# Long convolutions: taps of two channel tiles in turn, pair sums in column tiles, and two of the eight z units in the loop

## The chip, the cores and the metric

One core of one Trainium2 chip runs the kernel. The metric is the device time of one launch in microseconds (us); the median over the runs of the kernel before is given below. The engines are TensorE (PE in the rows), VectorE (DVE), ScalarE (ACT), GpSimd (POOL) and SyncE (SP), which issues the weight loads.

## The reference

The whole program is a chain of four mixers over x of 256 positions by 1024 channels, then a block of three attentions and a feed-forward part, all in float32. The change touches only the mixer of layers 0 and 3, the conformer convolution (E = 2048 inner channels, 31 taps):

```python
def conformer_conv_mixer(h, w_in, conv_w, conv_b, ln_g, ln_b, w_out):
    proj = h @ w_in
    val, glu_gate, z = jnp.split(proj, 3, axis=-1)
    u = val * jax.nn.sigmoid(glu_gate)
    u = causal_depthwise_conv(u, conv_w) + conv_b
    u = jax.nn.silu(layer_norm(u, ln_g, ln_b))
    return (u * jax.nn.silu(z)) @ w_out
```

The layer norm runs over the 2048 channels of a position, so its mean and variance are known only once all channels have been convolved.

## The kernel before

Channels lie on the 128 partitions and the 256 positions along the free axis, so the 2048 channels are 16 tiles (c = 0 to 15). Every engine has its own program and they meet by semaphores. The order of work is written out by hand in `conf_act`, `conf_pool`, `conf_dve` and `conf_pe`, once for each of the two convolutions (`j` = 0 and 1, called convolution 0 and 1 below).

**The loop.** For tile c PE computes the unit `vg[c]`: value and gate, 2 x 8 float32 matmuls of 256 columns (line 782; each is two passes, so two records in the trace). ACT takes the sigmoid of the gate (line 997) and DVE multiplies both into the padded buffer `up` (`gated`, line 1113). That multiply also frees the PSUM bank: `vg[c]` lies in bank 0 or 1, and the unit two places on takes the bank only then. The 31 taps are then split: DVE adds up 20 of them in two partial sums in a PSUM bank (lines 1141, 1139, 1144), ACT multiplies the other 11 (line 1026), through a ring of four buffers, and POOL adds these (line 1081), into `accp`, of which there are two. `join` adds the parts with two dependent additions (lines 1120 and 1121). From tile 3 on a `shift`, the mean of tile 0, goes into the partial sums to keep the variance accurate; tiles 0 to 2 get it afterwards (lines 1154, 1157).

**The sums.** For the layer norm PE multiplies a 128x128 block of ones by each convolved tile (line 1194, `sum_of`) and by its square from ACT (line 1200, `squares_of`): 32 float32 matmuls of 256 columns for a convolution, whose result stands in all 128 rows. DVE then works out mean and 1/std as 128x256 tiles (lines 1161 to 1172).

**z.** Eight units of z (2 x 8 matmuls each, line 782) are spread: one behind each of tiles 3, 7, 11 and 15, one among the last sums, and three (5, 6, 7) behind the last sum. ACT evicts them with silu (`conf_z`, line 976).

**The tail.** Tile by tile: DVE centres and scales (lines 1167, 1182), ACT takes silu (line 1052), POOL multiplies by silu(z) (line 1092), ACT writes the high part of y (line 955), DVE the low part (line 959). Behind z 7 PE starts the output product `out_pe` (lines 862 to 864, three one-pass matmuls for each k). Its first half-unit takes y tile by tile. An output unit is two half-units of 24 matmuls; for each, ACT must have copied the weights to `whi` (line 370) and DVE or POOL, by turns, must have written the rest to `wlo` (line 379). Four half-units fit into `whi`/`wlo`. In the tail ACT, POOL and DVE do these splits of the first units at fixed tiles: `AHEAD_BESIDE` and `OUT_BESIDE` put those of output unit 0 at tile 8, those of unit 1 and half of unit 2 at tile 13, and two more halves at tile 15. Units are loaded in the order of PE's use into a ring of three; a slot is loaded again once PE is through with it.

## Time and profile before

| | |
|---|---|
| median of 3 runs | 1503.85 us (1503.31 to 1507.31) |
| time of the profiled execution | 1504.31 us |
| its span, first to last instruction | 1502.5 us |
| mean granted TensorE clock | 0.998 |
| PE busy | 1476.4 us |
| DVE busy | 1074.9 us |
| ACT busy | 852.7 us |
| POOL busy | 499.7 us |

Busy time counts overlapping records once. Matmuls are pipelined, so the pace of a run of matmuls is read from the starts of two groups, not from the duration of one. In the timeline a row is a run of like instructions: start, time to the end of the last, engine, line, operation, tiles, count, and in brackets the idle time before it with the instruction that ended it.

### The profile page before, as it was taken

What the parts mean: (1) busy time and instruction counts of PE and PEld (TensorE: products, weight loads), DVE (VectorE), ACT (ScalarE), POOL (GpSimd) and SP (SyncE); (2) the same over time, 40 slices, a digit from 0 to 9 for tenths busy, and PEclk for the clock granted to TensorE, in tenths of its full rate; (3) what the DMA queues carried; (4) which work ended last, traced back from release to release, by engine and by line L of the source; (5) the groups of instructions that cost most, each with busy time, mean ns of one, the idle gap of its engine ahead of it and who ended that gap; (6) DMA issues with size and microseconds to landing.
All of it is one profiled execution on the core that took longest, in us unless ns stands there. A gap on an engine that the chain in (4) does not pass through costs nothing.

```text
span 1502.5 us, 25334 instructions
## 1 busy us (share of the span) xinstructions
PE 1476.4 (98%) x9411; PEld 1329.7 (88%) x9411; DVE 1074.9 (72%) x2235; ACT 852.7 (57%) x1604; POOL 499.7 (33%) x459
## 2 busy tenths in 40 slices
PE   8999999999999999999999999999999999999999
PEld 6888899998889988889988888989888878988887
DVE  5899966546787698887599997656247667786632
ACT  4676666545565555555456676545336655555542
POOL 2777642433333200000057785154421112000033
PEclk9999999999999999999999999999999999999999
DMA  7554454666644568866444444654753223576653
GB/s 206 149 148 139 139 197 157 223 173 150 138 144 142 157 187 210 218 196 196 144 136 141 141 141 162 189 141 134 214 153 93 78 85 113 168 197 190 177 191 116
DMA packets 308109, 239.40 MB, mean 159 GB/s; under 512 B 18017, under 2 KB 286707, under 8 KB 307988
## 3 DMA queue, kind: packets, MB, share of 16 engines
q1 hardware_dynamic: 295816, 228.70, 52.3%
q10 hardware_dynamic: 12172, 9.10, 2.6%
q8 instruction: 75, 1.23, 0.4%
q14 instruction: 46, 0.38, 0.1%
HBM read 236.02 MB, written 1.75 MB: 158 GB/s over the span
## 4 chain that ended last, share of the span: by engine, by line
PE 79%; DVE 14%; ACT 3%; SPq 1%; DMA 1%; issue 1%; POOL 1%; DVEq 0%; ACTq 0%; POOLq 0%
PE bank L782 15%; PE bank L802 12%; PE bank L804 6%; PE bank L862 3%; DVE bank L1144 3%; PE bank L864 3%; PE bank L863 3%; PE bank L1660 3%; PE bank L1662 3%; PE bank L1661 3%; PE bank L1287 2%; DVE wlo L379 2%; PE bank L825 2%; PE bank L761 1%; PE bank L763 1%; PE bank L762 1%
## 5 line engine op out<-in xcount | busy, mean ns | idle before, releaser
L379 POOL TENSOR_TENSOR wlo<-ring,whi 128x1024 fp32r<-128x1024 f32 x101 | 252.3, 2504 | 843.6 <-ACT whi L370 843.6
L370 ACT CAST whi<-ring 128x1024 fp32r<-128x1024 f32 x330 | 338.3, 1046 | 188.6 <-PE bank L1662 49.5
L379 DVE TENSOR_TENSOR wlo<-ring,whi 128x1024 fp32r<-128x1024 f32 (+1 forms) x229 | 291.6, 1293 | 150.8 <-ACT whi L370 150.1
L782 PE MATMUL bank<-sqb,ring 128*128 128x256 f32 x1504 | 330.3, 379 | 1.0 <-DMA ring<-in_a_w_in_dram 1.0
L782 PEld LDWEIGHTS bank<-sqb,ring 128*128 128x128 f32 x1504 | 285.7, 190 | 40.9 <-DMA ring<-in_a_w_in_dram 1.1
L802 PE MATMUL bank<-xhl,whi 128*128 128x512 f32 x768 | 269.1, 395 | 1.3 <-DVE xhl L707 1.3
L1081 POOL TENSOR_TENSOR scratch<-scratch 128x256 f32<-128x256 f32 x288 | 200.2, 732 | 107.3 <-ACT scratch L1026 96.6
L1144 DVE SCALAR_TENSOR_TENSOR bank<-scratch,convw,bank 128x256 f32<-128x256 f32 x576 | 231.1, 482 | 0.0
L804 PE MATMUL bank<-xhl,wlo 128*128 128x256 f32 x768 | 215.3, 280 | 0.0
L802 PEld LDWEIGHTS bank<-xhl,whi 128*128 128x128 f32 x768 | 144.0, 188 | 34.8 <-issue 2.1
L1026 ACT ACTIVATE scratch<-scratch,convw 128x256 f32<-128x256 f32 x320 | 144.2, 498 | 22.4 <-POOL scratch L1081 21.8
L862 PE MATMUL bank<-y_hi,whi 128*128 128x256 f32 x512 | 146.2, 286 | 2.4 <-POOL wlo L379 2.4
L804 PEld LDWEIGHTS bank<-xhl,wlo 128*128 128x128 f32 x768 | 145.3, 189 | 0.0
L863 PE MATMUL bank<-y_lo,whi 128*128 128x256 f32 x512 | 145.0, 283 | 0.0
L864 PE MATMUL bank<-y_hi,wlo 128*128 128x256 f32 x512 | 145.0, 283 | 0.0
L1660 PE MATMUL bank<-xhl,whi 128*128 128x256 f32 x384 | 110.3, 287 | 0.8 <-DVE qk L1620 0.8
L1661 PE MATMUL bank<-xhl,whi 128*128 128x256 f32 x384 | 108.7, 283 | 0.0
L1662 PE MATMUL bank<-xhl,wlo 128*128 128x256 f32 x384 | 108.6, 283 | 0.0
L862 PEld LDWEIGHTS bank<-y_hi,whi 128*128 128x128 f32 x512 | 98.3, 192 | 3.1 <-ACT whi L370 2.7
L863 PEld LDWEIGHTS bank<-y_lo,whi 128*128 128x128 f32 x512 | 98.3, 192 | 0.1
L864 PEld LDWEIGHTS bank<-y_hi,wlo 128*128 128x128 f32 x512 | 98.3, 192 | 0.0
L1335 ACT ACTIVATE scratch<-scratch,small 128x128 f32<-128x128 f32 (+1 forms) x120 | 50.9, 426 | 52.5 <-DVE small L1325 52.4
(312 smaller groups left out, 2891.5 us busy)
## 6 DMA issues: line engine op xcount, KB each, us to landing
ring<-in_a_w_in_dram SPq DMA_DIRECT2D x64, 512.0 KB, 5.1
ring<-in_b_w_in_dram SPq DMA_DIRECT2D x32, 1024.0 KB, 6.1
ring<-in_c_w_in_dram SPq DMA_DIRECT2D x64, 512.0 KB, 5.3
ring<-in_w_in_dram SPq DMA_DIRECT2D x26, 1024.0 KB, 5.3
ring<-in_w_ffn_in_dram SPq DMA_DIRECT2D x44, 512.0 KB, 5.0
ring<-in_a_w_in_dram SPq DMA_DIRECT2D x16, 1024.0 KB, 5.2
ring<-in_a_w_out_dram SPq DMA_DIRECT2D x16, 1024.0 KB, 5.0
ring<-in_w_ffn_out_dram SPq DMA_DIRECT2D x10, 1024.0 KB, 5.0
```

The source lines that it names most:

```text
L370: nc.scalar.copy(piece(whi, h)[:, :, 0:n], src).then_inc(hi_done, 1)
L379: engine.tensor_tensor(piece(wlo, h)[:, :, 0:n], src, piece(whi, h)[:, :, 0:n].bitcast(F32), ALU.subtract).then_inc(done, 1)
L782: mm = nc.tensor.matmul(o, halves[h][1][:, k, :], sqb[:, k, :], start=(k == 0), stop=(k == KD - 1))
L802: nc.tensor.matmul(o[:, :], wh[:, k, :], xhl[:, k, :, :].rearrange("p s t -> p (s t)"), start=(k == 0), stop=False, skip_group_check=True)
L804: mm = nc.tensor.matmul(o[:, 0:S], wl[:, k, :], xh[:, k, :], start=False, stop=(k == KD - 1), skip_group_check=True)
L862: nc.tensor.matmul(o, wh[:, k, :], hi[:, kk, :], start=first, stop=False, skip_group_check=True)
L863: nc.tensor.matmul(o, wh[:, k, :], lo[:, kk, :], start=False, stop=False, skip_group_check=True)
L864: mm = nc.tensor.matmul(o, wl[:, k, :], hi[:, kk, :], start=False, stop=end, skip_group_check=True)
L1081: nc.gpsimd.tensor_tensor(to, a, tmp[:, (first + i) % 4, :], ALU.add)\
L1144: ins = nc.vector.scalar_tensor_tensor(to[:, a, :], src, w, to[:, a, :], ALU.mult, ALU.add)
L1660: nc.tensor.matmul(o, wh, xh[:, k, :], start=first, stop=False, skip_group_check=True)
L1661: nc.tensor.matmul(o, wh, xl[:, k, :], start=False, stop=False, skip_group_check=True)
```

## The change

- Tiles 3 to 14 are convolved in pairs on DVE: the taps of two tiles by turns, one partial sum for each tile, so `join` is one addition a tile. The pair before is joined 12 taps into a pair, and the next two `gated` stand behind 16 and 34 of its 40 taps (the last, `gated(15)`, behind 34). `up` has four buffers instead of three. Tiles 0, 1, 2 and 15 stay single.
- ACT takes sigmoids a tile earlier (`SIGMOIDS`), the squares at other tiles (`SQUARES`), with three buffers instead of four.
- The sums of two tiles and of their two squares are four matmuls with 32 weight columns (a column of ones and 31 of zeros), to four groups of 32 rows of bank 7 (`pair_sums`, 8 for a convolution); they stand behind tiles 8, 10, 11, 13 and 15, behind z 2, and two inside z 5.
- ACT copies the sums to SBUF, PE transposes them, and DVE computes mean, variance and 1/std on 128x2 values. Two diagonal matrices and two matmuls with ones (`spread`) bring mean and 1/std back to all rows. All this stands at fixed places inside z 6.
- Two z units stay in the loop (behind tiles 10 and 14), six are behind it.
- In the tail DVE centres and scales two tiles with one instruction. The splits of output unit 0 stay at tile 8 and those of unit 1 at tile 13; those of unit 2 and later come behind tile 15.

```diff
                 n["z"].append((free, unit_in(w, [(2 * E + i * 2 * P, 2 * P)], plain=True)))
 
             for c in range(KE):
 
                 n["vg"].append((group((u_done, j * KE + c + 1)), unit_in(w, [(c * P, P), (E + c * P, P)], True, plain=(ph == 0 or c > 0))))
-                if c % 4 == 3:
-                    z_group(c // 4)
-            for i in range(4, 8):
+                if c in (10, 14):
+                    z_group((10, 14).index(c))
+            for i in range(2, 8):
...
-        Z_BESIDE = {6: 5, 10: 6, 13: 7}
-        AHEAD_BESIDE = {8: 6, 13: 7}
-        OUT_BESIDE = {13: 0, 15: 1}
+        Z_BESIDE = {6: 5, 11: 6, 15: 7}
+        OUT_BESIDE = {8: 0, 13: 1}
+        TILE_GROUPS = [(0,), (1,), (2,)] + [(c, c + 1) for c in range(3, KE - 1, 2)] + [(KE - 1,)]
+        SIGMOIDS = {0: (1,), 1: (2,), 2: (3, 4)} | {c: (c + 2,) for c in range(3, KE - 2)}
+        SQUARES = {3: (0,), 4: (1, 2)} | {c: (c - 2,) for c in range(5, KE)}
+        SUMS = {8: (0,), 10: (1,), 11: (2,), 13: (3,), KE - 1: (4,)}
+        Z_BEHIND = {10: 0, 14: 1}
+        one_column = cst[:, C_E1 + 15:C_E1 + 47]
+        x_sums = rr[:, 0:S]
+        l_sums = small[:, 208:212].rearrange("p (b s) -> p b s", b=TB)
+        l_negm, l_msq, l_var, l_rstd = (small[:, 212 + 2 * i:214 + 2 * i] for i in range(4))
+        l_warm = small[:, 220:221]
+        l_diag = [tmp[:, 2 * i:2 * i + 2, :].rearrange("p r w -> p (r w)")[:, 0:S] for i in range(2)]
+        stat_tr, stat_diag, stat_spread = sem("stat_tr"), sem("stat_diag"), sem("stat_spread")
...
 
         def conf_z(act, n, i):
 
@@ -984,8 +998,8 @@
                 rms_act(act, n["ph"])
 
...
-                if c % 4 == 0 and c:
-                    conf_z(act, n, c // 4 - 1)
+                if c == 12:
+                    conf_z(act, n, 0)
...
-                nc.scalar.activation(sq4[:, c % 4, :], yb[:, c, :], ACT.Square).then_inc(sqd_done, 1)
+                wait(act, sqm_done, j * (KE // 2) + (c - 3) // 2 + 1 if c >= 3 else 0)
+                nc.scalar.activation(csq[:, c % 3, :], yb[:, c, :], ACT.Square).then_inc(sqd_done, 1)
...
-                            conf_z(act, n, 3)
-                    if i == 2 * TAPS_POOL // 3 and c >= 3:
-                        square(c - 3)
+                        for s in SIGMOIDS.get(c, ())[0:1]:
+                            sigmoid(s)
+                        if c == KE - 2:
+                            conf_z(act, n, 1)
+                    if i == 2 * TAPS_POOL // 3:
+                        for s in SIGMOIDS.get(c, ())[1:]:
+                            sigmoid(s)
+                        for s in SQUARES.get(c, ()):
...
-            for c in range(KE - 3, KE):
+            for i in range(2, 5):
+                conf_z(act, n, i)
+            for c in range(KE - 2, KE):
                 square(c)
-            conf_z(act, n, 4)
+            nc.scalar.activation(l_warm, eps, ACT.Sqrt)
...
-                if c in AHEAD_BESIDE:
-                    act_ahead(act, n["z"][AHEAD_BESIDE[c]][1])
                 if c in OUT_BESIDE:
...
-                if c >= 3:
-                    wait(dve, tmp_done, (j * KE + c - 2) * TAPS_POOL)
-                nc.vector.tensor_tensor(up[:, c % 3, TAPS - 1:UPW], bank[g % 2][:, 0:S], sg[:, c % 2, :],
+                if c >= 4:
+                    wait(dve, tmp_done, (j * KE + c - 3) * TAPS_POOL)
+                nc.vector.tensor_tensor(up[:, c % 4, TAPS - 1:UPW], bank[g % 2][:, 0:S], csg[:, c % 2, :],
...
+            def join(gi):
+
+                cs = TILE_GROUPS[gi]
+                for a, c in enumerate(cs):
+                    done = raw_done if c < 3 else conv_done
+                    dve.wait_ge(pool_sum, j * KE + c + 1)
+                    dve.wait_ge(step, ended[gi][a])
+                    if len(cs) == 2:
+                        nc.vector.tensor_tensor(yb[:, c, :], acc[gi % 2][:, a, :], accp[:, c % 2, 0, :], ALU.add).then_inc(done, 1)
+                        continue
+                    chain(dve, nc.vector.tensor_tensor(yb[:, c, :], acc[gi % 2][:, 0, :], accp[:, c % 2, 0, :], ALU.add))
+                    dve.wait_ge(step, ended[gi][1])
+                    nc.vector.tensor_tensor(yb[:, c, :], acc[gi % 2][:, 1, :], yb[:, c, :], ALU.add).then_inc(done, 1)
...
-            for c in range(KE + 1):
...
+            for gi, cs in enumerate(TILE_GROUPS):
+                for c in cs:
...
-                    for k in range(TAPS_DVE):
-                        if k == 2 * TAPS_DVE // 3 and c + 1 < KE:
-                            gated(c + 1)
-                            dve_ahead(dve, n["vg"][c + 1][1])
...
+                pair = len(cs) == 2
+                to = acc[gi % 2]
+                prev = [None, None]
+                for i in range(TAPS_DVE * len(cs)):
+                    a = i % 2
+                    k, c = (i // 2, cs[a]) if pair else (i, cs[0])
+                    if pair and i == 12:
+                        join(gi - 1)
+                        if c == 3:
+                            shifted(2)
+                    if pair and i == 16 and cs[0] + 3 < KE:
+                        gated(cs[0] + 2)
+                    if pair and i == 34:
+                        gated(cs[0] + 3 if cs[0] + 3 < KE else cs[0] + 2)
+                    if c < 2 and i == (17, 13)[c]:
+                        gated(c + 1)
+                    if c == 2 and i == 7:
+                        gated(3)
+                    if c == KE - 1 and i == 8:
+                        join(gi - 1)
...
+                if gi in (1, 2):
+                    if gi == 2:
+                        gated(4)
+                    join(gi - 1)
...
+            join(len(TILE_GROUPS) - 1)
+            dve.wait_ge(stat_tr, j + 1)
+            sums = bank[7][:, 0:S].rearrange("p (b s e r) -> p b s e r", b=TB, s=2, e=2)[:, :, :, :, 0]
+            chain(dve, nc.vector.tensor_reduce(l_sums, sums, AX, ALU.add))
+            chain(dve, nc.vector.tensor_scalar(l_negm, l_sums[:, :, 0], -1.0 / E, None, ALU.mult))
+            chain(dve, nc.vector.tensor_tensor(l_msq, l_negm, l_negm, ALU.mult))
+            nc.vector.scalar_tensor_tensor(l_var, l_sums[:, :, 1], 1.0 / E, l_msq, ALU.mult, ALU.subtract).then_inc(var_done, 1)
+
+            def diagonal(i, col):
+                for tb in range(TB):
+                    nc.vector.tensor_scalar(l_diag[i][:, tb * P:(tb + 1) * P], ident, col[:, tb:tb + 1], None, ALU.mult).then_inc(stat_diag, 1)
+
+            diagonal(0, l_negm)
+            dve.wait_ge(lstd_done, j + 1)
+            chain(dve, nc.vector.reciprocal(l_rstd, l_var))
+            diagonal(1, l_rstd)
...
+            def centre(q):
+                nc.vector.tensor_tensor(yb[:, 2 * q:2 * q + 2, :], yb[:, 2 * q:2 * q + 2, :], both(3), ALU.add).then_inc(dc_done, 1)
...
+            dve.wait_ge(stat_spread, 2 * j + 1)
+            for q in range(2):
+                centre(q)
+            dve.wait_ge(stat_spread, 2 * j + 2)
+            for q in range(KE // 2 + 2):
+                if q + 2 < KE // 2:
+                    centre(q + 2)
+                if q < KE // 2:
+                    dve.wait_ge(dc_done, j * (KE // 2) + q + 1)
+                    nc.vector.tensor_tensor(yb[:, 2 * q:2 * q + 2, :], yb[:, 2 * q:2 * q + 2, :], both(2), ALU.mult).then_inc(dn_done, 1)
+                for c in (2 * q - 1, 2 * q):
+                    if c in OUT_BESIDE:
+                        lo_dve_to(dve, last(n["out"][OUT_BESIDE[c]][2]))
+                for c in (2 * q - 3, 2 * q - 2):
+                    if 0 <= c < KE:
+                        y_low(dve, n["y0"] + c, y_hi[:, c, :], y_lo[:, c, :])
             out_dve(dve, n)
...
-            def sum_of(c):
-                pe.wait_ge(conv_done, j * KE + c + 1)
-                mm = nc.tensor.matmul(bank[7][:, 0:S], ones, yb[:, c, :], start=(c == 0), stop=(c == KE - 1))
...
-            def squares_of(c):
-                pe.wait_ge(sqd_done, j * KE + c + 1)
-                nc.tensor.matmul(bank[6][:, 0:S], ones, sq4[:, c % 4, :], start=(c == 0), stop=(c == KE - 1)).then_inc(sqm_done, 1)
+            def pair_sums(q):
+                pe.wait_ge(conv_done, j * KE + 2 * q + 2)
+                pe.wait_ge(sqd_done, j * KE + 2 * q + 2)
+                srcs = [yb[:, 2 * q, :], yb[:, 2 * q + 1, :], csq[:, 2 * q % 3, :], csq[:, (2 * q + 1) % 3, :]]
+                for i, src in enumerate(srcs):
+                    mm = nc.tensor.matmul(bank[7][32 * i:32 * i + 32, 0:S], one_column, src, start=(q == 0), stop=(q == KE // 2 - 1))
+                mm.then_inc(sqm_done, 1)
+
+            def stats_turned():
+                pe.wait_ge(mean_done, j + 1)
+                nc.tensor.transpose(bank[7][:, 0:P], x_sums[:, 0:P], ident)
+                nc.tensor.transpose(bank[7][:, P:S], x_sums[:, P:S], ident).then_inc(stat_tr, 1)
+
+            def spread(i):
+                pe.wait_ge(stat_diag, 4 * j + 2 * i + 2)
+                nc.tensor.matmul(bank[3 - i][:, 0:S], ones, l_diag[i], start=True, stop=True).then_inc(stat_spread, 1)
 
             for c in range(KE):
...
-                if c % 4 == 3:
-                    i = c // 4
-                    if i:
-                        pe.wait_ge(sz_done, j * 8 + i)
+                for q in SUMS.get(c, ()):
+                    pair_sums(q)
+                if c in Z_BEHIND:
+                    i = Z_BEHIND[c]
+                    wait(pe, sz_done, j * 8 + i if i else 0)
                     proj_T(pe, *n["z"][i], at=z_bank(n, i))
-                if c >= 4:
-                    sum_of(c - 4)
-                if c >= 6:
-                    squares_of(c - 6)
-            sum_of(KE - 4)
-            squares_of(KE - 6)
-            proj_T(pe, *n["z"][4])
-            sum_of(KE - 3)
-            squares_of(KE - 5)
-            squares_of(KE - 4)
-            sum_of(KE - 2)
-            squares_of(KE - 3)
-            sum_of(KE - 1)
-            for c in range(KE - 2, KE):
-                squares_of(c)
-            for i in range(5, 8):
-                proj_T(pe, *n["z"][i])
+            proj_T(pe, *n["z"][2])
+            pair_sums(5)
+            proj_T(pe, *n["z"][3])
+            pe.wait_ge(sz_done, j * 8 + 2)
+            proj_T(pe, *n["z"][4], at=z_bank(n, 4))
+            pe.wait_ge(shift_done, j + 1)
+            proj_T(pe, *n["z"][5], at=z_bank(n, 5), at_k={(0, 3): lambda: pair_sums(6), (1, 4): lambda: pair_sums(7)})
+            proj_T(pe, *n["z"][6], at_k={(0, 1): stats_turned, (0, 5): lambda: spread(0), (0, 7): lambda: spread(1)})
+            proj_T(pe, *n["z"][7])
             out_pe(pe, n, y_hi, y_lo, KE, y_split, n["y0"])
```

The three places at which the order of instructions matters most:

DVE before, one tile of the steady loop, from the first tap of a tile to its predecessor's join (L1139/L1141/L1144 are taps, L1113 is `gated`, L1120/L1121 the join):

```order
L1141 TENSOR_SCALAR bank<-scratch,convw 128x256
L1139 SCALAR_TENSOR_TENSOR bank<-scratch,convw,bank 128x256
L1144 SCALAR_TENSOR_TENSOR bank<-scratch,convw,bank 128x256 x11
L1113 TENSOR_TENSOR scratch<-bank,scratch 128x256
L1144 SCALAR_TENSOR_TENSOR bank<-scratch,convw,bank 128x256 x7
L1120 TENSOR_TENSOR wide<-bank,scratch 128x256
L1121 TENSOR_TENSOR wide<-bank,wide 128x256
```

DVE after, one pair of tiles (L1185/L1190 are taps, L1130 is `gated`, L1144 the join):

```order
L1185 SCALAR_TENSOR_TENSOR bank<-scratch,convw,bank 128x256 x2
L1190 SCALAR_TENSOR_TENSOR bank<-scratch,convw,bank 128x256 x10
L1144 TENSOR_TENSOR wide<-bank,scratch 128x256 x2
L1190 SCALAR_TENSOR_TENSOR bank<-scratch,convw,bank 128x256 x4
L1130 TENSOR_TENSOR scratch<-bank,scratch 128x256
L1190 SCALAR_TENSOR_TENSOR bank<-scratch,convw,bank 128x256 x18
L1130 TENSOR_TENSOR scratch<-bank,scratch 128x256
L1190 SCALAR_TENSOR_TENSOR bank<-scratch,convw,bank 128x256 x6
```

Two tiles were 40 taps, 2 `gated` and 4 additions; a pair is 40 taps, 2 `gated` and 2 additions.

PE before, from behind z 4 to the output product (L782 are the matmuls of z 5, 6 and 7, L1194 and L1200 the sums, L862 the output product):

```order
L1194 MATMUL bank<-wide,cst 128x256 [waits conv_done]
L1200 MATMUL bank<-scratch,cst 128x256 [waits sqd_done] x2
L1194 MATMUL bank<-wide,cst 128x256 [waits conv_done]
L1200 MATMUL bank<-scratch,cst 128x256 [waits sqd_done]
L1194 MATMUL bank<-wide,cst 128x256 [waits conv_done]
L1200 MATMUL bank<-scratch,cst 128x256 [waits sqd_done] x2
L782 MATMUL bank<-sqb,ring 128x256 [waits unit_loaded0,u_done]
...
L862 MATMUL bank<-y_hi,whi 128x256 [waits y_split,lo_dve,hi_done]
```

PE after, from the last pair of sums, inside z 5, to the end of z 6 (L783 the matmuls of z, L1255 `pair_sums`, L1260 and L1261 the transposes, L1265 `spread`):

```order
L1255 MATMUL bank<-scratch,cst 32x256 x2
L783 MATMUL bank<-sqb,ring 128x256 x3
L783 MATMUL bank<-sqb,ring 128x256 [waits unit_loaded1,sz_done]
L783 MATMUL bank<-sqb,ring 128x256
L1260 MATMUL bank<-cst,rr 128x128 [waits mean_done]
L1261 MATMUL bank<-cst,rr 128x128
L783 MATMUL bank<-sqb,ring 128x256 x4
L1265 MATMUL bank<-scratch,cst 128x256 [waits stat_diag]
L783 MATMUL bank<-sqb,ring 128x256 x2
L1265 MATMUL bank<-scratch,cst 128x256 [waits stat_diag]
L783 MATMUL bank<-sqb,ring 128x256 [waits unit_loaded1]
```

Three whole z units stood between the last sum and the output product; now it is one unit, half of another and what stands between the sums and `spread`.

ACT before, at tile 13 of the tail and behind it (L976 is z 7, L370 the weight copies, L1052 silu, L955 the high part of y):

```order
L976 ACTIVATE wide<-bank 128x512
L370 CAST whi<-ring 128x1024 x3
L1052 ACTIVATE wide<-wide,cols 128x256
L955 CAST y_hi<-yr 128x256
L1052 ACTIVATE wide<-wide,cols 128x256
L955 CAST y_hi<-yr 128x256
L370 CAST whi<-ring 128x1024 x2
```

ACT after, the same place (L371 the weight copies, L1071 silu, L958 the high part, L990 z 7):

```order
L371 CAST whi<-ring 128x1024 x2
L1071 ACTIVATE wide<-wide,cols 128x256
L958 CAST y_hi<-yr 128x256
L1071 ACTIVATE wide<-wide,cols 128x256
L958 CAST y_hi<-yr 128x256
L990 ACTIVATE wide<-bank 128x512
L1071 ACTIVATE wide<-wide,cols 128x256
L958 CAST y_hi<-yr 128x256 x2
L371 CAST whi<-ring 128x1024 x9
```

The first half of output unit 2 was copied at tile 13; it is now copied behind the last y.

## Rows read from the trace of the kernel before

**Rows 1.** The page, busy time of PE and weight loads:

```profile
PE 1476.4 (98%) x9411; PEld 1329.7 (88%) x9411; DVE 1074.9 (72%) x2235; ACT 852.7 (57%) x1604; POOL 499.7 (33%) x459
```

**Rows 2.** Groups by line, the two kinds of sums, both convolutions:

```profile
L1194 PE MATMUL bank<-wide,cst 128*128 128x256 f32 x64 | 19.4, 384 | 0.6 <-DVE wide L1121 0.6
L1200 PE MATMUL bank<-scratch,cst 128*128 128x256 f32 x64 | 18.4, 379 | 0.0
```

**Rows 3.** Waits of PE: total, times, longest:

```profile
PE bank L862 <- POOL wlo L379: 2.4, 2, 1.6
```

**Rows 4.** Timeline of PE, convolution 0: vg 4's start, a tile, z 5, output:

```profile
44.23 13.98 PE L782 MATMUL bank<-sqb,ring 128*128 128x256 f32 x64
...
65.81 7.07 PE L782 MATMUL bank<-sqb,ring 128*128 128x256 f32 x32
72.72 0.59 PE L1194 MATMUL bank<-wide,cst 128*128 128x256 f32 x2
73.15 0.59 PE L1200 MATMUL bank<-scratch,cst 128*128 128x256 f32 x2
...
176.08 20.88 PE L782 MATMUL bank<-sqb,ring 128*128 128x256 f32 x96
196.61 0.47 PE L862 MATMUL bank<-y_hi,whi 128*128 128x256 f32 x1
```

**Rows 5.** Timeline of DVE, a steady tile, and two additions without dependence:

```profile
49.00 0.75 DVE L1154 TENSOR_TENSOR wide<-wide,bank 128x256 f32<-128x256 f32 x2
...
118.57 0.42 DVE L1120 TENSOR_TENSOR wide<-bank,scratch 128x256 f32<-128x256 f32 x1
119.02 0.42 DVE L1121 TENSOR_TENSOR wide<-bank,wide 128x256 f32<-128x256 f32 x1
...
127.65 0.42 DVE L1120 TENSOR_TENSOR wide<-bank,scratch 128x256 f32<-128x256 f32 x1
```

**Rows 6.** Timeline of PE: 32-column matmuls elsewhere, two column groups, 512 columns wide:

```profile
274.53 0.28 PE L1662 MATMUL bank<-xhl,wlo 128*128 128x256 f32 x1
274.74 1.91 PE L1656 MATMUL bank<-scratch,cst 128*32 128x512 f32 x8
276.58 0.29 PE L1732 MATMUL bank<-cst,scratch 16*128 16x16 f32 x2
```

**Rows 7.** Timelines of ACT and POOL: four tap products, z's table loads, skew's DMAs, eight adds:

```profile
50.33 1.28 ACT L976 ACT_TABLE_LOAD   x1
51.62 0.60 ACT L976 ACTIVATE wide<-bank 128x512 f32<-128x512 f32 x1
...
61.05 1.69 ACT L1026 ACTIVATE scratch<-scratch,convw 128x256 f32<-128x256 f32 x4
70.06 7.32 ACTq L1060 DMA_DIRECT2D skew<-qk  x3
66.50 5.53 POOL L1081 TENSOR_TENSOR scratch<-scratch 128x256 f32<-128x256 f32 x8 [0.30 <-ACT scratch L1026]
```

**Rows 8.** Timeline of PE, convolution 1: start of z 0, start of the output:

```profile
774.34 13.98 PE L782 MATMUL bank<-sqb,ring 128*128 128x256 f32 x64
926.71 0.47 PE L862 MATMUL bank<-y_hi,whi 128*128 128x256 f32 x1
```

**Rows 9.** Timeline of DVE, first norm: small sum, reciprocal, two diagonal blocks:

```profile
8.03 0.16 DVE L647 TENSOR_TENSOR small<-small 128x2 f32<-128x2 f32 x1
8.75 0.48 DVE L652 TENSOR_SCALAR qk<-cst,small 128x128 f32<-128x128 f32 x2
```

**Rows 10.** Timelines of ACT, DVE and POOL, tail of convolution 0:

```profile
182.00 1.26 ACT L1052 ACTIVATE wide<-wide,cols 128x256 f32<-128x256 f32 x2 [2.44 <-DVE wide L1182]
189.61 1.99 ACT L370 CAST whi<-ring 128x1024 fp32r<-128x1024 f32 x2
199.81 1.99 ACT L370 CAST whi<-ring 128x1024 fp32r<-128x1024 f32 x2
190.68 1.23 DVE L379 TENSOR_TENSOR wlo<-ring,whi 128x1024 fp32r<-128x1024 f32 x1 [2.24 <-ACT whi L370]
191.67 2.44 POOL L379 TENSOR_TENSOR wlo<-ring,whi 128x1024 fp32r<-128x1024 f32 x1 [1.61 <-ACT whi L370]
```

**Rows 11.** Windows, PE: busy, count, granted clock, DMA, around 1030 us:

```profile
1030.00:1036.00 6.00, 6.00 (x58) 0.78 0.56 175
```

125 lines of the change are left out of this document (47 added, 78 removed).

## The prediction

> **What bounds the kernel now.** I read the page first: PE is busy 1476.4 of 1502.5 us, the others 33 to 72% [rows 1]. So only three things count: work taken from PE or given to it, gaps that PE gets, gaps that it loses. The groups by line give the work in question: 64 records for each kind of sum, with almost no waiting before them [rows 2]. The waits of PE show that its only wait of size in the convolutions is for a `wlo` split in the output product: 2.4 us in two places, the longest 1.6 [rows 3]. The timelines then give the paces. A unit of 2 x 8 float32 matmuls takes 72.72 - 65.81 = 6.91 us and one matmul of a sum 73.15 - 72.72 = 0.43 [rows 4]. DVE needs 127.65 - 118.57 = 9.08 us for a tile in the steady loop; less a join of 0.91 (0.45 to the second addition, 0.46 to its successor) and `gated` at 0.33 (two independent additions in 0.75, of which the last runs on for 0.42) that is 7.84 for 20 taps, 0.39 a tap [rows 5]. PE before gives a tile 6.91 + 0.86 for sums + 1.7 for its share of z = 9.5 us, so it hides a DVE of 9.1. That cover is what the change uses up.
>
> **PE's work, one convolution.** Removed: 32 x 0.43 = 13.8 us, and 0.3 of waiting for the last joins. Added: eight `pair_sums`. No row shows four column groups in turn, but eight records for two groups of 32 columns and 512 positions took 276.58 - 274.74 = 1.84 us [rows 6]. One after another they would take 8 x 0.43 (twice a 0.216 us pass of 256) = 3.4, so each two ran together; the edges cost 0.09 (0.21 instead of 0.12 ahead, as much behind). If four run together, a `pair_sums` costs 2 x 0.216 + 0.18 = 0.61; if two, 1.05; if none, 1.9. I take 0.61, since the two groups start together there as four would here: 4.9 us. Two transposes (0.21 each), two `spread` (0.43 each) and their edges: 1.5. Net 13.8 + 0.3 - 4.9 - 1.5 = 7.7 us a convolution, were PE never to wait.
>
> **It will wait in the loop.** Six z units leave it, so PE asks for tiles every 6.9 us while DVE still takes 8.5: a pair is 40 x 0.39 + 2 x 0.33 for `gated` + 2 x 0.33 for the joins = 17.0 us. I follow convolution 0. `vg[4]` starts at 44.23 [rows 4] and ends at 51.14, now right behind tile 3. DVE's pairs start 3.3 us later, since ACT has the sigmoid (0.4), four products (1.7, [rows 7]) and the shift (0.4) to do before DVE's two shift additions (0.67): 54.4. The first pair takes 17.6 (chained join and tile 2's shift), four more 68.0. Silu of z 0 costs ACT two table loads and an eviction, 1.28 + 0.60 + 1.28 [rows 7], just ahead of sigmoid 12, which DVE wants 3.1 us after ACT gets there: 0.5 us late. Pair (13, 14) starts at 140.5, `gated(15)` stands behind 34 taps and a join: 154.5, done at 154.9. z 3 takes the bank that `gated(15)` frees. PE comes to z 3 after 15 units and six `pair_sums`: 44.23 + 103.7 + 3.7 = 151.5. **So it waits 3.4 us there.** POOL takes 5.53 for eight adds [rows 7], some 7.3 a tile, and may start a pair's first tile only once the pair before is joined, 5 us into the pair: done at 5.2 + 14.6 = 19.8, wanted at 21.7. That is close but hidden; if the cover of 1.9 us goes, DVE and then z 3 are late by the rest. The skew DMAs hold ACT for 7.32 us from 70.06 [rows 7]; sigmoid 7 then comes at 78.8, wanted at 79.0: hidden.
>
> From z 3 on PE has five units, two `pair_sums` and 1.5: 155.0 + 34.6 + 1.2 + 1.5 = 192.3 for the start of the output product, against 196.6 [rows 4]. Convolution 1 starts the same stretch at 774.34 and has its output at 926.71 [rows 8], 926.71 - 774.34 = 152.4 us as in convolution 0 (196.61 - 44.23): the same 4.3 us. **Gain ahead of the output: 2 x 4.3 = 8.6 us.**
>
> **The tail has less time.** Before, z 5, 6 and 7 (20.5 us) lay between the last sum and the output. Now it is 2.2 us from the last `pair_sums` to the transposes (u below), then 14.3 to the output. The statistics fit between the k of z 6: the first norm did a small sum, root, reciprocal and two diagonal blocks in 8.03 to 9.23 [rows 9]; with three more small steps the diagonals are ready at u + 2.0 and u + 2.7, PE comes to them at u + 2.2 and u + 3.5. No wait there. The second `spread` is through at u + 4.1; centring and scaling two tiles (0.6 to 0.7 each, twice a tile's 0.33) give ACT its first silu at u + 5.5. From first silu to the weight copies of output unit 0 it took 189.61 - 182.00 = 7.6 us [rows 10], and ACT has the same list now: u + 13.1. The half is ready 1.0 + 1.3 us later if DVE splits it (convolution 0), 1.0 + 2.5 if POOL does (convolution 1, where the parity is turned): u + 15.4 and u + 16.6, while PE is there at u + 14.3. First waits 1.1 and 2.3.
> Unit 1: before, 199.81 - 189.61 = 10.2 us lay between the copies of units 0 and 1 [rows 10]. Less z 7 (0.6), which moves behind, and some waits for DVE, whose scaling is in pairs, I get 9: PE wants unit 1 at u + 21.2 and 22.4; it is split at u + 24.4 and 26.5: waits 3.2 and 4.1. Unit 2: its first half is now copied behind tile 15's y, 5.9 us of ACT and POOL work after unit 1's copies: waits 2.0 and 1.1. Behind that splits (1.0 for ACT, 1.23 or 2.44 for DVE or POOL, [rows 10]) outrun the 2.88 us of a half again. Sum 6.3 and 7.5; the 0.8 and 1.6 of before [rows 3] go: **+5.5 and +5.9, loss 11.4 us.** Bounds: ACT alone, never waiting, would have unit 1 copied 2.5 us sooner, which leaves 3 us a convolution; with each wait for POOL and DVE as before it is 8.
>
> **Sum:** -8.6 + 11.4 = +2.8 against the profiled execution's 1504.31, which is 0.5 above the median; rounded, 1506.5 for the median.
>
> **Rivals.**
> *A, the tail keeps up.* If the y chain and the splits are as early as in ACT's bound and POOL's splits don't hold up y, the tail loses 0 to 3 us a convolution: 1503.85 - 8.6 + 2 = 1497, or 1495 at best. For it: DVE and POOL stood idle for 2.24 and 1.61 us ahead of their first splits [rows 10], so they have room. Against: unit 1 was already 1.6 late in one convolution [rows 3] with 5.6 us more time. Chance 0.29.
> *B, slower: PE's clock falls in the new gaps.* The trace has a stretch with a granted clock of 0.78, that is 2.6 of 6 us at 1.2 instead of 2.4 GHz, behind nothing worse than matmuls of 30 columns [rows 11]. Each such spell costs 1.3 us. The waits at z 3 and at unit 1 are 3 to 4 us of idle PE, longer than any in the trace before: four places, 5.2 us, 1511.5. It decides if at least two of the four waits bring the clock down. Against: the gap of 1.6 us did not. Chance 0.15. The Trainium skill ("TensorE: Matmul & The Clock Gate", Part 1) says that the clock is halved after idle stretches and comes back only with sustained work; by that rule the time is this rival's 1511.5 instead of 1506.5; the trace so far has no gap long enough to test it.
> *C, the column groups don't overlap.* Then a `pair_sums` costs 1.9; those ahead of z 3 vanish in its wait, the two behind it cost 2.6 a convolution: 1511.7. The eight records of [rows 6] speak against it. Chance 0.04.
> *D, the loop isn't held by DVE* (PE does not wait at z 3): 7 us less, 1499.5. It needs DVE below 0.31 us a tap. Chance 0.04.
>
> **Numbers.** My case 0.48, 1502 to 1509.5 by itself. Range 1495 to 1512: it takes in A and B. A run of this kernel tells about 0.3% (4.5 us) from no change. Faster by more: A but for its slow end, and D: 0.29. Slower by more: B, C and my case's upper end: 0.23. Within: 0.48.
>
> **What would show it.** After: groups of four 32-column matmuls starting together; DVE at 17 us a pair; a wait of 3 to 4 us on PE ahead of z 3, in both convolutions, for `gated`; output starts 4 us after or before 192 and 922 mean that the loop is mis-sized. Then waits of L865 for `wlo` of 5 to 8 us a convolution; none would be A. Granted clock below 1 behind a gap would be B. Wrong altogether if POOL is late for the joins or PE waits for the diagonals inside z 6.

## The result and the profile after

| | before | after |
|---|---|---|
| median of 20 runs each | 1504.33 us (1503.03 to 1509.36) | 1511.49 us (1507.31 to 1513.97) |
| profiled execution | 1504.31 us | 1508.22 us |
| its span, mean granted clock | 1502.5 us, 0.998 | 1506.4 us, 0.994 |

The ratio of after to before is 1.0037, 95% interval 1.0029 to 1.0045: slower, by a little: 4.4 to 6.8 us. (The medians alone lie 7.2 us apart, the means 5.9; the text goes by the ratio.) My case had given 1506.5, with 1502 to 1509.5 for itself. The median lies 5 us above 1506.5, above my case's own stretch and 0.5 us inside the whole range; by the ratio the time is about 1509.5. It is close to rival B's number (1511.5), but not by rival B's way, as shown below.

The page of after, busy times, then shares of the chain that ended last:

```profile
PE 1468.7 (97%) x9423; PEld 1311.8 (87%) x9423; DVE 1057.3 (70%) x2189; ACT 843.5 (56%) x1600; POOL 500.1 (33%) x459
PE 65%; DVE 23%; issue 6%; ACT 3%; POOL 2%; DMA 1%; SPq 0%; POOLq 0%; DVEq 0%; ACTq 0%
```

PE is busy 7.7 us less than in [rows 1] over the whole kernel, and the span is 3.9 us longer: PE now waits. Its waits (total, times, longest) say for what:

```profile
PE bank L783 <- DVE scratch L1130: 4.7, 3, 2.2
PE bank L865 <- DVE wlo L380: 3.9, 2, 2.3
...
PE bank L865 <- POOL wlo L380: 2.6, 2, 2.1
PE bank L865 <- issue: 2.3, 1, 2.3
...
PE bank L865 <- ACT whi L371: 1.4, 1, 1.4
PE bank L865 <- DVE y_lo L962: 1.4, 2, 0.9
```

L865 is the output product; of such waits [rows 3] had 2.4 us in all, here it is 11.6. The row with "issue" names no releaser: it is the wait ahead of the first output matmul of convolution 1, which starts at 927.23, and POOL's split of that half-unit ends at 927.13 (924.78 + 2.35). L783 is z 3, which waits for `gated` (L1130). PE's timeline in convolution 0: vg 4, one `pair_sums`, the wait ahead of z 3, the transposes, the output product's start, and its waits ahead of units 1 and 2:

```profile
43.06 17.21 PE L783 MATMUL bank<-sqb,ring 128*128 128x256 f32 x79
...
77.69 0.41 PE L1255 MATMUL bank<-wide,cst 128*32 128x256 f32 x2
77.70 0.41 PE L1255 MATMUL bank<-scratch,cst 128*32 128x256 f32 x2
77.93 0.39 PE L1255 MATMUL bank<-wide,cst 128*32 128x256 f32 x2
77.94 0.39 PE L1255 MATMUL bank<-scratch,cst 128*32 128x256 f32 x2
78.25 2.00 PE L783 MATMUL bank<-sqb,ring 128*128 128x256 f32 x8
...
151.27 0.39 PE L1255 MATMUL bank<-scratch,cst 128*32 128x256 f32 x2
153.90 2.43 PE L783 MATMUL bank<-sqb,ring 128*128 128x256 f32 x10 [2.25 <-DVE scratch L1130]
...
177.12 0.27 PE L1260 MATMUL bank<-cst,rr 128*128 128x128 f32 x1
...
180.80 10.52 PE L783 MATMUL bank<-sqb,ring 128*128 128x256 f32 x48
192.72 0.36 PE L865 MATMUL bank<-y_hi,whi 128*128 128x256 f32 x1 [1.40 <-ACT whi L371]
...
202.22 0.36 PE L865 MATMUL bank<-y_hi,whi 128*128 128x256 f32 x1 [1.62 <-DVE wlo L380]
...
210.52 0.55 PE L865 MATMUL bank<-y_hi,whi 128*128 128x256 f32 x1 [2.31 <-DVE wlo L380]
210.87 0.41 PE L866 MATMUL bank<-y_lo,whi 128*128 128x256 f32 x1
211.08 0.42 PE L867 MATMUL bank<-y_hi,wlo 128*128 128x256 f32 x1
```

In a `pair_sums` the four groups start within 0.02 us of each other in each pass, and from the first of them to the next matmul of z it is 78.25 - 77.69 = 0.56 us. That is not its whole cost: the first starts 0.31 us behind the last matmul of z ahead of it, and the second matmul of z behind it 0.32 us after the first, where 0.22 is the pace. With these edges a `pair_sums` costs 0.77 us.

One reference point serves for before and after: m0's product, PE's matmul of ones with tile 0 (line 1215 before, 1280 after), from which the shift comes. The unit right behind it is z 0 before the change ([rows 4] and the prediction call it vg 4) and vg 4 after it. From that unit the output product starts 192.72 - 43.06 = 149.7 us on, against 152.4 in [rows 4]; 1.6 us of that is the new wait at its head, so PE was there 4.3 us sooner. Then the output product, which was through in 47 us from its first matmul, takes 54 (table below). The last two rows show a matmul every 0.21 us where 0.12 is the pace: the clock has halved behind the wait. The windows of after (PE's busy time and count, the other engines', then granted clock, DMA share, GB/s) around that place, the two others in the second output product, and a stage with no wait:

```profile
206.00:216.00 10.00, 7.70 (x53) 7.52 (x52) 4.93 (x5) 6.09 (x9) 7.26 (x4) 0.83 0.52 178
920.00:930.00 10.00, 7.69 (x36) 6.79 (x35) 7.90 (x13) 7.12 (x15) 6.54 (x7) 0.86 0.62 200
934.00:946.00 12.00, 9.37 (x64) 9.02 (x64) 7.83 (x8) 8.56 (x14) 9.18 (x6) 0.86 0.26 87
600.00:640.00 40.00, 40.00 (x233) 34.98 (x232) 32.64 (x54) 21.71 (x37) 0.00 (x0) 1.00 0.86 213
```

The first three windows have a granted clock of 1.00 before the change.

Two ways to give the length of a wait occur below. The brackets give the idle time as the profile has it. A gap is the time from the start of one matmul to the start of the next, which is 0.3 to 0.4 us more: 2.31 in brackets ahead of unit 2 is a gap of 2.6, and 1.40 ahead of the output product is a gap of 1.8.

What the convolutions took, from the starts of PE's rows (first value convolution 0, second convolution 1):

| us | before | after |
|---|---|---|
| the unit behind m0's product to PE's arrival at the output product | 152.4, 152.4 | 148.1, 148.0 |
| arrival to the last output matmul | 47.4, 48.0 | 55.3, 54.6 |
| of that the cost of half clock | 0, 0 | 1.4, 3.0 |

(The half-unit of 24 matmuls from 210.52, at half clock, took 4.26 us to the start of its last; the same one in experiment 8, at full clock, took 2.83.) So 8.7 us were gained ahead of the output and 14.5 lost in it. The rest of the 3.9 us between the profiled executions is outside the change: m0's product started 1.2 us sooner and what follows convolution 1 took 0.7 us less.

### The profile page after: what moved, and what is told of

Read it like the earlier page. It is cut to its first block, busy times and chain, and to the rows that moved or that the text cites. A ratio compares the mean times of both kernels' runs of the same rounds, so it can differ in the third digit from the quotient of the medians.

```text
span 1506.4 us, 25346 instructions
## 1 busy us (share of the span) xinstructions
PE 1468.7 (97%) x9423; PEld 1311.8 (87%) x9423; DVE 1057.3 (70%) x2189; ACT 843.5 (56%) x1600; POOL 500.1 (33%) x459
## 4 chain that ended last, share of the span: by engine, by line
PE 65%; DVE 23%; issue 6%; ACT 3%; POOL 2%; DMA 1%; SPq 0%; POOLq 0%; DVEq 0%; ACTq 0%
PE bank L805 12%; DVE bank L1190 11%; PE bank L807 6%; PE bank L865 3%; PE bank L866 3%; PE bank L867 3%; PE bank L1718 3%; PE bank L1720 3%; PE bank L1719 3%; PE bank L783 3%; DVE wlo L380 2%; PE bank L1345 2%; PE bank L828 2%; PE bank L787 1%; PE bank L886 1%
## 5 line engine op out<-in xcount | busy, mean ns | idle before, releaser
L371 ACT CAST whi<-ring 128x1024 fp32r<-128x1024 f32 x330 | 338.6, 1046 | 199.3 <-PE bank L1720 49.5
L783 PE MATMUL bank<-sqb,ring 128*128 128x256 f32 x1504 | 331.9, 381 | 5.5 <-DVE scratch L1130 4.7
L783 PEld LDWEIGHTS bank<-sqb,ring 128*128 128x128 f32 x1504 | 284.0, 190 | 51.9 <-DVE scratch L1130 7.9
L805 PE MATMUL bank<-xhl,whi 128*128 128x512 f32 x768 | 269.1, 396 | 1.4 <-DVE xhl L708 1.4
L1190 DVE SCALAR_TENSOR_TENSOR bank<-scratch,convw,bank 128x256 f32<-128x256 f32 x600 | 240.9, 489 | 0.0
L807 PE MATMUL bank<-xhl,wlo 128*128 128x256 f32 x768 | 213.9, 279 | 0.0
L805 PEld LDWEIGHTS bank<-xhl,whi 128*128 128x128 f32 x768 | 144.2, 188 | 36.1 <-issue 2.1
L865 PE MATMUL bank<-y_hi,whi 128*128 128x256 f32 x512 | 148.4, 290 | 11.7 <-DVE wlo L380 3.9
L807 PEld LDWEIGHTS bank<-xhl,wlo 128*128 128x128 f32 x768 | 144.6, 188 | 0.0
L865 PEld LDWEIGHTS bank<-y_hi,whi 128*128 128x128 f32 x512 | 100.5, 196 | 13.6 <-ACT whi L371 6.8
```

The lines of the kernel that those rows point to most:

```text
L371: nc.scalar.copy(piece(whi, h)[:, :, 0:n], src).then_inc(hi_done, 1)
L783: mm = nc.tensor.matmul(o, halves[h][1][:, k, :], sqb[:, k, :], start=(k == 0), stop=(k == KD - 1))
L805: nc.tensor.matmul(o[:, :], wh[:, k, :], xhl[:, k, :, :].rearrange("p s t -> p (s t)"), start=(k == 0), stop=False, skip_group_check=True)
L807: mm = nc.tensor.matmul(o[:, 0:S], wl[:, k, :], xh[:, k, :], start=False, stop=(k == KD - 1), skip_group_check=True)
L865: nc.tensor.matmul(o, wh[:, k, :], hi[:, kk, :], start=first, stop=False, skip_group_check=True)
L1190: ins = nc.vector.scalar_tensor_tensor(to[:, a, :], src, w, to[:, a, :], ALU.mult, ALU.add)
```

## The experiments

Each ratio is to the kernel before, run on the same chip in the same turn.

**1. The gate alone.** `gated(15)` stands behind 34 taps of the last pair; here behind 24.

```diff
-                    if pair and i == 34:
+                    if pair and i == (34 if cs[0] + 3 < KE else 24):
```

> The changed kernel, but the last gated (tile 15) stands behind 24 taps of the pair (13, 14) instead of 34; nothing else differs. My theory: the wait of 2.3 us ahead of z 3 is for this one multiply, and since the last sums stand at fixed places in PE's program, everything behind them comes earlier by the length of the wait: 2 x 2.3 = 4.6 us less than the changed kernel's 1511.5, so about 1507, with no wait ahead of z 3 and the waits in the output product as long as before. Rival (the tail is tied to the end of DVE's taps, not to PE's order): the wait only moves behind z 7, no gain, 1511.5.

Measured: 1505.29 us, ratio 1.0001 (0.9991 to 1.0011), so 0.0036 below after, 5.4 us. The wait ahead of z 3 is gone in both convolutions; the output product's waits are the same to 0.1 us in the first. The z 3 waits cost what they last: from m0's product to the first output matmul it takes 147.75 us in convolution 0 and 148.66 in 1, against 150.09 and 150.99 in after. That is 2.3 us each, as the bracket at 153.90 has it, and 4.7 of the 5.4; the interval takes in the rest.

**2. The statistics sooner.** One pair of sums moves into z 4, the other to z 5's start, transposes and `spread` into z 5; ACT squares tiles 14 and 15 ahead of silu of z 4.

```diff
-            proj_T(pe, *n["z"][4], at=z_bank(n, 4))
+            proj_T(pe, *n["z"][4], at=z_bank(n, 4), at_k={(0, 3): lambda: pair_sums(6)})
-            ... z 5: {(0, 3): pair_sums(6), (1, 4): pair_sums(7)}
-            ... z 6: {(0, 1): stats_turned, (0, 5): spread(0), (0, 7): spread(1)}
+            ... z 5: {(0, 0): pair_sums(7), (0, 5): stats_turned, (1, 1): spread(0), (1, 3): spread(1)}
```

> The changed kernel with the last two pair sums, the transposes and the spreads 12 to 13 matmuls earlier: pair sums 6 inside z 4, 7 behind the first matmul of z 5, transposes and spreads inside z 5; ACT takes the last two squares ahead of evicting z 4. My theory: the output product waits because the statistics are late by PE's own order (DVE has its last tile at 167.7 us, PE sums it at 174.6), so starting them 5.2 us sooner takes about 5 us of waiting out of each output product, and without long gaps the clock no longer falls (another 1.3 to 2.7 us): 1511.5 - 10 - 3, about 1498. Rival (the splits by ACT and POOL alone bound the output product, whenever the statistics come): waits of 5 us stay, no gain over 1 us.

Measured: 1500.19 us, ratio 0.9967 (0.9954 to 0.9981). This edit takes nothing from PE's work and gives back 0.007, 10 us; the cover between sums and output was what the change lacked. In convolution 0 the transposes come 129.3 us behind m0's product instead of 134.5. ACT's order was changed in the same run, so it doesn't say what either does by itself. Its waits of PE:

```profile
PE bank L783 <- DVE scratch L1131: 4.5, 2, 2.3
...
PE bank L865 <- POOL wlo L380: 3.0, 2, 2.0
PE bank L865 <- DVE wlo L380: 2.3, 1, 2.3
```

**3. Both.** 

> Both edits together. My theory: the gains add up, as the one moves the whole stretch and the other shortens what is left of it: 1498 - 4.6 = about 1493.5, faster than the kernel before the change (1504.3) by 0.7%. Rival (a tail tied to DVE's end): as the statistics alone or slower.

Measured: 1502.32 us, ratio 0.9976 (0.9965 to 0.9988): a miss, and no better than 2 alone. PE's timeline in z 4:

```profile
158.80 1.46 PE L783 MATMUL bank<-sqb,ring 128*128 128x256 f32 x6
162.38 0.41 PE L1256 MATMUL bank<-wide,cst 128*32 128x256 f32 x2 [2.12 <-ACT scratch L1022]
```

PE, no longer held at z 3, comes to the moved sums before the squares of tiles 12 and 13 are there: the wait had only moved, 2.1 us twice. The squares of a pair are the next input in the chain, and the edit had not moved them.

**4. The kernel before, with less cover.** z 5 runs ahead of the last sums instead of behind them.

```diff
             proj_T(pe, *n["z"][4])
+            proj_T(pe, *n["z"][5])
...
-            for i in range(5, 8):
+            for i in range(6, 8):
```

> The kernel before the change with z 5 moved ahead of the last sums, so that two z units instead of three lie between the last sum and the output product; PE's work is the same. My theory: the chain from the statistics to the split y and weights needs all of the 20.5 us, so taking 6.9 us of them away costs 6 to 7.5 us in each output product, and the clock falls in the gaps: 1504.3 + 13 + 1 to 4, about 1519. Rival (the loss in the changed kernel comes from its other parts: pairs in the tail, later splits of unit 2, column sums): less than 3 us, 1504 to 1507.

Measured: 1518.08 us, ratio 1.0076 (1.0061 to 1.0090). Not one instruction is added, and a z unit on the wrong side of the last sum costs 11 us. Its largest wait is another than the one that I meant:

```profile
PE bank L782 <- ACT wide L976: 9.7, 2, 4.9
```

Its timelines of ACT and PE in convolution 0:

```profile
194.73 0.59 ACT L976 ACTIVATE wide<-bank 128x512 f32<-128x512 f32 x1
...
195.37 8.86 PE L782 MATMUL bank<-sqb,ring 128*128 128x256 f32 x32 [4.86 <-ACT wide L976]
```

PE waits 4.9 us, in both convolutions, ahead of z 7, for ACT to empty the bank of z 5; ACT does that only at tile 6 of the tail (194.73), where its program has it. The output product itself takes 47.5 us from its first matmul in both convolutions, against 47.4 and 48.0 before. So the number came near 1519 by another mechanism than my theory's, which had the loss in the output product. The run shows that z units behind the last sum cover the start of the tail; it does not size the change's own waits, and my theory's 6 to 7.5 us in each output product is not shown.

**5. Unit 2's split sooner.** Its first half is split beside tile 13, as before the change.

```diff
-                    hi_to(act, last(n["out"][OUT_BESIDE[c]][2]))
+                    hi_to(act, last(n["out"][OUT_BESIDE[c]][2]) + (c == 13))
```

and so for DVE's and POOL's low parts.

> The changed kernel, with one edit: the first half of output unit 2's weights is split beside tile 13, together with unit 1's halves, instead of behind tile 15. Theory (the tail of statistics, SiLU and weight splits is now too short, and its last piece is unit 2's first half): the waits ahead of output unit 2, 2.6 us in the first convolution and 0.8 us in the second, go, and the spell at half clock that followed the first of them goes too, so some 3 to 5 us less than the changed kernel, a ratio to the kernel before of about 1.001. Rival (the tail's engines are full, and an earlier split only moves the wait): tile 13 comes later by the split's 2.5 us on GpSimd, a wait of that size stands ahead of a later product instead, and the ratio stays at 1.003 to 1.005.

Measured: 1508.16 us, ratio 1.0019 (1.0006 to 1.0032), between the two numbers. Its trace has no gap ahead of unit 2, but in the first convolution one of 1.7 us ahead of its second half, instead of 2.6 ahead of the first, with no half clock behind it; in the second there is none. So part of the wait went and part moved on by a half-unit.

**6. 2 and 5 together.** 

> The changed kernel with the statistics started sooner (as in stats_early) and the first half of output unit 2 split beside tile 13. Theory: what stats_early left in the output products, a wait of 2.6 us ahead of unit 2 in the first convolution and 2.3 us in the second with the half-clock spells behind them, goes: ratio to the kernel before 0.994 to 0.995, about 1496 to 1498. Rival (the split only moves its wait): as stats_early, 0.9967.

Measured: 1497.43 us, ratio 0.9949 (0.9933 to 0.9965), inside the theory's 0.994 to 0.995. It is not told apart from experiment 2, whose interval (0.9954 to 0.9981) overlaps. The waits ahead of unit 2 are gone, but here too a gap of 1.7 us stands ahead of its second half in the first convolution.

**7. Each step where its input is ready.** 1, 5 and the statistics sooner, with the sums later than in 3.

```diff
+            ... z 4: {(1, 2): pair_sums(6)}
+            ... z 5: {(0, 4): pair_sums(7), (1, 1): stats_turned, (1, 5): spread(0), (1, 7): spread(1)}
```

> The changed kernel with tile 15 gated earlier, unit 2's first half split beside tile 13, and the statistics started sooner but with each step placed where the vector engine has its input ready when TensorE comes by: sums 6 in the second half of z 4, sums 7 in the first half of z 5, the turned sums in its second half, the spreads at its end. Theory: neither the wait ahead of z 3 (2.6 us, twice) nor the one ahead of sums 6 that both_early had (2.5 us, twice) is left, and the output waits are those of stats_early_unit2_sooner or 1 to 2 us more each: ratio 0.990 to 0.993, about 1490 to 1494. Rival: statistics that start 2.5 us later than in both_early give the waits back in the output product: ratio 0.996 to 0.998.

Measured: 1494.01 us, ratio 0.9933 (0.9913 to 0.9954), just above the theory's 0.990 to 0.993, which its interval takes in, and clear of the rival's 0.996. No wait is left at z 3 or in z 4; what is left stands in the output product:

```profile
PE bank L865 <- POOL wlo L380: 4.1, 2, 2.7
...
PE bank L865 <- DVE wlo L380: 1.6, 1, 1.6
```

This is the fastest kernel of the study; its interval overlaps that of 6.

**8. The gaps filled.** The same kernel as after, with 24 products more.

```diff
+            for _ in range(n.get("fill", {}).get(i, 0)):
+                nc.tensor.matmul(b[:, 0:S], ones, l_diag[0], start=True, stop=True, skip_group_check=True)
...
+            n["fill"] = ({0: 4, 1: 4, 2: 5}, {0: 5, 1: 5, 2: 1})[j]
```

> The changed kernel with idle TensorE time filled and nothing else changed: ahead of output units 0, 1 and 2 TensorE runs 4, 4 and 5 (first convolution) and 5, 5 and 1 (second) extra products of 256 columns at 0.43 us whose result nothing reads (the unit's first product starts its bank anew), about the length of the waits there. Theory (the clock falls to half behind a gap of 2.4 us or more, at 1.3 us or more a time): the spells inside the output products go, some 3 to 4 us off the changed kernel: ratio to the kernel before 1.001 to 1.002. Rival (the spells have nothing to do with the gaps, and the waits alone set the time): the ratio stays at 1.0037 or rises by up to 0.001, since the extra products overrun their gaps a little.

Measured: 1511.10 us, ratio 1.0037 (1.0022 to 1.0051), the ratio of after itself: the time that I expected did not come. But the clock did. Windows over both output products:

```profile
190.00:215.00 25.00, 23.56 (x164) 21.76 (x163) 18.89 (x20) 17.54 (x30) 16.64 (x14) 1.00 0.41 133
928.00:950.00 22.00, 19.13 (x134) 17.34 (x133) 15.72 (x19) 15.26 (x27) 15.67 (x12) 1.00 0.43 144
```

The mean granted clock over its runs is 0.9965, against 0.9938 for after and 0.997 for before. Why so little gain? In the first convolution there is one: from m0's product to the last output matmul it takes 202.4 us instead of 203.8, the 1.4 of the one stretch there. That is 0.0009 of the ratio, which its interval can't show. In the second convolution the last wait, ahead of unit 2, ends at the same distance from m0's product in both. Of after, then of this kernel:

```profile
776.24 0.70 PE L1280 MATMUL bank<-wide,cst 128*128 128x256 f32 x2 [0.18 <-DVE wide L1148]
944.80 0.36 PE L865 MATMUL bank<-y_hi,whi 128*128 128x256 f32 x1 [0.54 <-POOL wlo L380]
```

```profile
778.19 0.70 PE L1282 MATMUL bank<-wide,cst 128*128 128x256 f32 x2 [0.18 <-DVE wide L1150]
948.42 0.35 PE L867 MATMUL bank<-y_hi,whi 128*128 128x256 f32 x1 [1.57 <-POOL wlo L380]
```

168.6 us, and 170.2, of which 1.7 is a stretch at half clock in z 3 that this execution had and after's had not. The split comes when it comes; matmuls at half clock ahead of it only shorten the wait for it (0.54 us left, 1.57 without them). Of after's three stretches in the output products only the one behind the last wait of its convolution, from 210.52 on, costs time. Experiment 1's trace agrees: its convolution 1 has no stretch behind the first wait, and the wait ahead of unit 1 is 2.77 instead of 2.09 us, while the output product takes the same 52.1 us from its first matmul. My theory's threshold, a gap of 2.4 us or more, does not hold: the gaps ahead of z 3 are 2.6 us in after, with no half clock behind either.

**9. Splits in the order of need.** Output units 0 to 3 read tiles 0 to 7 only, so units 1 and 2 are wanted before tiles 10 to 15.

```diff
-        OUT_BESIDE = {8: 0, 13: 1}
+        OUT_BESIDE = {8: 0, 10: 1, 13: 2}
```

> The changed kernel with one line changed: output units 0, 1 and 2 are split beside tiles 8, 10 and 13 (instead of 0 beside 8, 1 beside 13, 2 behind 15). The first four output units read tiles 0 to 7 alone, so TensorE needs unit 1's and 2's splits before it needs tiles 10 to 15. Theory (it is the order of the tail's work, more than its amount, that makes TensorE wait ahead of units 1 and 2): the waits ahead of unit 1 (1.9 and 2.4 us) and unit 2 (2.6 and 0.8 us) go with the clock spell behind one of them, the wait for unit 0's split ahead of the first product stays: 7 to 9 us less than the changed kernel, ratio to the kernel before 0.998 to 0.999. Rival (the tail's amount of work decides): tiles 8 to 15 come later by what the splits took, unit 4 waits for them, and the ratio stays at 1.002 to 1.004.

Measured: 1512.80 us, ratio 1.0050 (1.0032 to 1.0068). Both theories missed: the wait came inside unit 0. DVE's and POOL's timelines, then PE's:

```profile
197.84 1.22 DVE L380 TENSOR_TENSOR wlo<-ring,whi 128x1024 fp32r<-128x1024 f32 x1 [0.82 <-ACT whi L371]
198.98 2.90 DVE L962 TENSOR_TENSOR y_lo<-yr,y_hi 128x256 fp32r<-128x256 f32 x2
...
198.83 2.44 POOL L380 TENSOR_TENSOR wlo<-ring,whi 128x1024 fp32r<-128x1024 f32 x1 [1.72 <-ACT whi L371]
```

```profile
201.60 0.58 PE L865 MATMUL bank<-y_hi,whi 128*128 128x256 f32 x1 [5.09 <-DVE y_lo L962]
```

DVE's program had tile 7's low half behind unit 1's split, which itself waited for its weights. That is not all of the 5.1 us: the low half of tile 7, 0.41 us by itself, took 2.57 (198.98 to 201.55) while POOL had its own split running until 201.27, which makes some 2.2 us of the wait. The last section has more on this. The same line in kernel 7:

> The kernel all_three_in_step with output units 0, 1 and 2 split beside tiles 8, 10 and 13. Theory: its waits ahead of unit 1 and 2 (1.9 and 1.7 us in the first convolution, 2.9 us in the second with a half-clock spell of 1.4 us behind it) go: ratio to the kernel before 0.988 to 0.990, about 1487 to 1490. Rival: later tiles 8 to 15 hold up unit 4 instead, ratio 0.992 to 0.994 as all_three_in_step.

Measured: 1500.67 us, ratio 0.9966 (0.9953 to 0.9978), with the same wait, gaps of 4.2 us twice. It misses the theory's 0.988 to 0.990 and the rival's 0.992 to 0.994 too.

**10. Beside tile 11.** `OUT_BESIDE = {8: 0, 11: 1, 13: 2}` puts the low halves of tiles 7 and 8 ahead of the split. In after, and in kernel 7:

> The changed kernel with output units 0, 1 and 2 split beside tiles 8, 11 and 13. In splits_by_need the vector engine's order put unit 1's split (beside 10) ahead of tile 7's low half, which TensorE wants next, and TensorE waited 5.4 us there; beside 11 the low halves of tiles 7 and 8 stand ahead of it. Theory (the order of the tail's work makes the waits ahead of units 1 and 2): those waits (7.7 us in both convolutions) and the spell behind one go now, ratio to the kernel before 0.998 to 1.000. Rival (the amount decides: the three engines take what they take for tiles and splits, in whatever order): as unit2_sooner, 1.001 to 1.003.

Measured: 1506.91 us, ratio 1.0007 (0.9989 to 1.0025).

> The kernel all_three_in_step with output units 0, 1 and 2 split beside tiles 8, 11 and 13. Theory: its waits of 1.9 and 1.7 us in the first convolution and 2.9 us in the second go: ratio to the kernel before 0.988 to 0.990, about 1488 to 1490. Rival: waits of that size elsewhere, 0.992 to 0.994.

Measured: 1497.20 us, ratio 0.9941 (0.9922 to 0.9961). The gaps ahead of unit 1 shrank (0.6 us is left in one convolution of the first kernel, 1.2 in one of the second, both with the pace of 0.1 in them), but gaps of 2.6 and 2.1 us stand later, ahead of unit 3. Both the order and the amount of the tail's work decide; neither kernel is told apart from its neighbour, unit2_sooner or kernel 7.

## Why the prediction was right, and where it was off

- **PE's work.** The four column groups run together, so rival C is out. But a `pair_sums`, put at 0.61 with its edges, costs 0.77, and the sum of 7.7 us less per convolution is too large. Kernel 7 has no wait of size ahead of its output product and comes to it 188.64 - 42.65 = 146.0 us behind m0's product, against 196.61 - 43.80 = 152.8 before: 6.8 us less. The forecast of the gain did not suffer, since the wait at z 3 took up the difference. Of before, then of kernel 7:

```profile
43.80 0.59 PE L1215 MATMUL bank<-wide,cst 128*128 128x256 f32 x2
```

```profile
42.65 0.59 PE L1281 MATMUL bank<-wide,cst 128*128 128x256 f32 x2
...
188.64 0.47 PE L865 MATMUL bank<-y_hi,whi 128*128 128x256 f32 x1
```

- **The wait in the loop.** z 3 was to start 155.0 - 44.23 = 110.8 us after vg 4; it did at 153.90 - 43.06 = 110.8. PE came 1.5 us later than worked out, mostly by the dearer `pair_sums`, so the wait was 2.3, not 3.4. Experiment 1 shows it to cost its length. DVE takes 104.78 - 87.80 = 17.0 us a pair, as forecast. Right; rival D is out. Starts of two pairs in after:

```profile
87.80 0.88 DVE L1185 SCALAR_TENSOR_TENSOR bank<-scratch,convw,bank 128x256 f32<-128x256 f32 x2
...
104.78 0.88 DVE L1185 SCALAR_TENSOR_TENSOR bank<-scratch,convw,bank 128x256 f32<-128x256 f32 x2
```

- **Gain ahead of the output.** 8.6 predicted, 8.7 measured. It hangs on when `gated(15)` comes, and that was right to 0.1 us. PE does not wait for the diagonals inside z 6, nor DVE for POOL at the joins, as forecast.
- **The tail.** First silu at u + 5.5 predicted, 182.32 - 177.12 = 5.2 measured; copies of unit 0 at u + 13.1, measured 13.2; of unit 1 at u + 22.1, measured 22.7:

```profile
182.32 1.09 ACT L1071 ACTIVATE wide<-wide,cols 128x256 f32<-128x256 f32 x2 [2.38 <-DVE wide L1236]
...
190.32 1.99 ACT L371 CAST whi<-ring 128x1024 fp32r<-128x1024 f32 x2
...
199.78 1.99 ACT L371 CAST whi<-ring 128x1024 fp32r<-128x1024 f32 x2
```

  The step that was off is the size of this loss, "+5.5 and +5.9, loss 11.4 us". Output stages without half clock lost 6.5 and 3.6 by the table; but experiment 8 shows that in the second convolution the slow matmuls only took the place of waiting, so its own loss is the whole 6.6: 13.1 us in all. The single waits are further off than their sum. In convolution 0 the waits for the splits of units 0, 1 and 2 were put at 1.1, 3.2 and 2.0 us and the gaps less the pace are 1.6, 1.8 and 2.5; what I had put at nothing are the waits for y's low halves inside unit 0 (1.4 us in the page, 1.7 as gaps less the pace), which made PE later at unit 1 and its wait there shorter. That the sum comes near is in part luck.
- **The clock.** I gave rival B 0.15 and its price 5.2 us. The clock did fall: three stretches in the profiled execution. But of the four waits that I had named, at z 3 and unit 1, only one had a stretch behind it, and only one of the three stretches, 1.4 us, adds to the time. So rival B as I had it did not decide, and that the median is its 1511.5 is chance. Its price of 1.3 a spell was read from a window that ends at 1036.00, inside the spell (the next window of before, 1036 to 1046, has 0.96). Together: -8.7 + 13.1 + 1.4 = +5.8 us. The ratio says +4.4 to +6.8. So of the missing 3 us, 1.7 is the tail and 1.4 the clock; that split is worked out from the traces of after and experiment 8, one execution each, and no median isolates it.
- **Rival A** did not happen as the change stands, but experiments 2, 6 and 7 show its mechanism: with the transposes 3.5 to 5.8 us sooner behind m0's product the tail keeps up but for one or two splits in each convolution. That 6 measured 1497, rival A's number, says little: its interval is 5 us wide, and its trace has two half-clock stretches behind the waits at z 3, which rival A's sum did not have.

## What to carry to other kernels

Before work is taken from the bound engine, find what that work covers: here PE's work fell by some 13.6 us in all, and the units that moved behind the loop did not lie between the statistics and the product that waits for them. Place each step of a side chain where its input is ready when the bound engine comes by, and once one wait is removed, look at the next step for the same wait (experiment 3); in a queue, what stands ahead of the wanted instruction counts as much as what it waits for (experiment 9). In the traces of experiments 1 and 8 a slower clock ahead of a later wait cost nothing, and behind the last wait it cost in full.
